# Strips for the modulation rows' products, and an earlier layer boundary, in a two-layer diffusion backbone on one core

## What is computed

```python
for l in range(2):
    mod = silu(c) @ w_mod[l] + b_mod[l]            # 6 x 1024 numbers for each of the two groups
    h = rmsnorm(x) * (1 + mod[1]) + mod[0]
    branches = gmlp(h), conv(h), rwkv_scan(h), attention(h)     # from h @ w_in
    mix = sum_n sigmoid(h @ w_gate[n]) * (branch_n @ w_branch[n]) @ w_out
    x = x + mod[2] * mix
    h = rmsnorm(x) * (1 + mod[4]) + mod[3]
    x = x + mod[5] * moe(h)                        # 16 experts, 2 for each token
y = rmsnorm(x) * final_g
```

## Time and profile before

| | |
|---|---|
| time, median of 3 runs | 2992.97 us (2980.88 to 2995.16) |
| the profiled execution | 2981.84 us, its span 2980.2 us |
| PE busy | 2491.1 us (84%) |
| DVE busy | 1338.7 us (45%) |
| ACT busy | 938.7 us (31%) |
| mean DMA rate | 153 GB/s |
| first product of layer 1 | at 1447.68 us |

### The profile page before, as it was taken

How to read it: one execution, slowest core, us unless ns; L and a number is a source line. 1 busy time by engine, 2 the same in 40 slices (tenths; PEclk the granted TensorE clock), 3 DMA queues, 4 the chain that set the end, 5 groups by cost and what they waited for, 6 DMA issues and landing times. The chain is left out here.

```text
span 2980.2 us, 40890 instructions
## 1 busy us (share of the span) xinstructions
PE 2491.1 (84%) x16436; PEld 1845.7 (62%) x16436; DVE 1338.7 (45%) x1680; ACT 938.7 (31%) x1272; POOL 144.4 (5%) x142
## 2 busy tenths in 40 slices
PE   5998888899987985988569988899889979858880
PEld 2785576667665674777238756676667646747770
DVE  1226433332234644888332283323332255458873
ACT  3122332222121123777221313312222111247771
POOL 0000000100000001000100000001000000010001
PEclk8999899999998996999779998999999989779995
DMA  7117211120113504999532372102111044069984
GB/s 300 57 62 279 93 51 71 70 73 24 64 60 129 209 23 180 395 397 399 230 118 85 122 248 74 72 15 75 69 71 45 35 164 166 29 258 395 395 338 179
DMA packets 75071, 455.78 MB, mean 153 GB/s; under 512 B 8544, under 2 KB 24928, under 8 KB 44384
## 3 DMA queue, kind: packets, MB, share of 16 engines
q1 hardware_dynamic: 57888, 347.10, 30.6%
q0 software_dynamic: 8928, 72.97, 6.5%
q10 hardware_dynamic: 8064, 33.03, 2.7%
HBM read 387.02 MB, written 92.27 MB: 161 GB/s over the span
## 5 line engine op out<-in xcount | busy, mean ns | idle before, releaser
L782 PE MATMUL ps<-h,ring 128*128 128x320 f32 x2048 | 622.6, 455 | 25.0 <-ACT mod_cols L1324 12.8
L782 PEld LDWEIGHTS ps<-h,ring 128*128 128x128 f32 x2048 | 391.9, 197 | 194.9 <-issue 35.5
L782 PE MATMUL ps<-arena 64*64 64x64 f32 (+3 forms) x6608 | 390.0, 249 | 48.2 <-DVE arena L1810 14.3
L782 PEld LDWEIGHTS ps<-arena 64*64 64x64 f32 (+2 forms) x6608 | 297.9, 145 | 169.8 <-issue 135.2
L2041 DVE TENSOR_TENSOR we_lo<-arena,we_hi 128x2048 fp32r<-128x2048 f32 x150 | 339.4, 2290 | 91.7 <-ACT we_hi L1487 91.7
L1487 ACT CAST we_hi<-arena 128x2048 fp32r<-128x2048 f32 x150 | 282.8, 1912 | 2.7 <-DMA arena<-in_experts 2.4
L785 PE MATMUL ps<-fix,arena 128*128 128x128 f32 x836 | 136.1, 308 | 169.3 <-DMA arena<-expert_rows 58.8
L785 PEld LDWEIGHTS ps<-fix,arena 128*128 128x128 f32 x836 | 109.8, 158 | 196.9 <-DVE arena L2071 60.2
L782 PE MATMUL ps<-ring,small 128*2 128x512 f32 x384 | 179.0, 622 | 35.1 <-DMA ring<-in_stream 21.4
L1832 DVE TENSOR_TENSOR arena<-arena,ps 128x512 f32<-128x512 f32 x50 | 34.4, 688 | 355.9 <-PE ps L782 355.9
L782 PE MATMUL ps<-wz_hi,hz_hi 128*128 128x512 f32 (+1 forms) x480 | 181.2, 377 | 15.6 <-DVE hz_lo L1582 15.6
(11 more groups left out here) (286 smaller groups left out, 3399.9 us busy)
## 6 DMA issues: line engine op xcount, KB each, us to landing
arena<-in_experts SPq DMA_DIRECT2D x150, 1024.0 KB, 8.9
ring<-in_stream SPq DMA_DIRECT2D x58, 2048.0 KB, 7.7
arena<-expert_rows SPq DMA_DIRECT2D x50, 512.0 KB, 7.2
expert_out<-rows ACTq DMA_DIRECT2D x50, 512.0 KB, 8.3
gates<-arena SPq DMA_DIRECT2D x128, 160.0 KB, 1.8
ring<-gates SPq DMA_DIRECT2D x16, 1280.0 KB, 5.4
arena<-in_wbranch POOLq DMA_DIRECT2D x2, 3584.0 KB, 12.1
x_kept<-x ACTq DMA_DIRECT2D x2, 2560.0 KB, 15.2
```

What stands on the lines that cost most here:

```text
L782: return nc.tensor.matmul(out, lhsT, rhs, start=start, stop=stop)
```

## The change

It does these things:

- The stationary operand of the modulation products becomes 32 columns wide (`cP`, 2 of them filled, zeroed once), and tile k writes the 32 PSUM partitions of strip k mod 4, so that neighbouring products lie in different column strips of the array. Each strip sums two tiles. ACT copies all 128 partitions; `mod_columns` turns them with a constant `strips` that adds the four strips, a product over 128 rows instead of 2.
- At the start of a layer PE works through all four `w_mod` slots before it turns the first one, and each has its own `mod_row`; ACT copies four times and then adds four biases.
- `cols` and `rows` of the first layer are loaded at once; those of the next layer `cols` after the scatter to the experts and `rows` after the gathers, both on POOL's queue (also after the last layer, where they hold zeros).
- x is stored and squared block by block, behind the addition that completes the block, at the end of the layer before.
- `round_in(1)` and `rest_in(1)` move into the middle of `h_scaled`, and `hz_done` comes in two halves, so that PE needs only the first for the first half slot.
- In the tail the final scale releases one output DMA for each block, and `final_g` is loaded behind `rows`; ACT waits for the last `x_kept` before the root.

```diff
-    "hz_done": 1, "whi_done": 2 * (SLOTS_IN + SLOTS_OUT), "wlo_done": 2 * (SLOTS_IN + SLOTS_OUT),
+    "hz_done": 2, "whi_done": 2 * (SLOTS_IN + SLOTS_OUT), "wlo_done": 2 * (SLOTS_IN + SLOTS_OUT),
...
-    "params_loaded": 2 * 16, "x_kept": 16, "cache_out": 2 * 16, "state_stored": 16, "x_back": 16, "wb0_loaded": 16, "wb1_loaded": 16,
+    "params_loaded": 2 * 16, "x_kept": NB * 16, "cache_out": 2 * 16, "state_stored": 16, "x_back": 16, "wb0_loaded": 16, "wb1_loaded": 16,
...
+cP = sb("silu_c_padded", KT * STRIP)[:, :].rearrange("p (k g) -> p k g", k=KT)
...
-mod_row = combT_t[0:2, 0:512]
+mod_row = [arena[:, 8192 + i * 512:8192 + (i + 1) * 512] for i in range(SLOTS_MOD)] + [combT_t[:, 0:512]] * (MODS - SLOTS_MOD)
...
 def _(pool):
...
+    pool.dma_start(cols[:, :], a["cols"][0]).then_inc(params_loaded, 16)
+    pool.dma_start(rows[:, :], a["rows"][0].broadcast_to([P, NROWS])).then_inc(params_loaded, 16)
...
-        pool.wait_ge(x_done, now.value("x_done", 0))
-        pool.sem_inc(waits_settled, 1)
-        pool.dma_start(cols[:, :], a["cols"][pick].rearrange("o p c -> (o p) c")).then_inc(params_loaded, 16)
-        pool.dma_start(rows[:, :], a["rows"][pick].rearrange("o p c -> (o p) c").broadcast_to([P, NROWS])).then_inc(params_loaded, 16)
...
+        after = bass.ds(layer + 1, 1)
+        pool.dma_start(cols[:, :], a["cols"][after].rearrange("o p c -> (o p) c")).then_inc(params_loaded, 16)
+        pool.wait_ge(params_loaded, now.value("params_loaded", 48))
+        pool.sem_inc(waits_settled, 1)
...
-    pool.wait_ge(x_done, 1 + DEPTH * PER["x_done"])
+        pool.dma_start(rows[:, :], a["rows"][after].rearrange("o p c -> (o p) c").broadcast_to([P, NROWS])).then_inc(params_loaded, 16)
-    pool.wait_ge(final_done, 1)
-    yv = arena[:, 0:NB * D].rearrange("p (b d) -> p b d", b=NB)
-    pool.dma_start(a["y_prompt"], yv[:, 0]).then_inc(cache_out, 16)
-    pool.dma_start(a["y_sample"].rearrange("(b p) d -> p b d", p=P), yv[:, 1:NB]).then_inc(cache_out, 16)
-    pool.wait_ge(cache_out, DEPTH * PER["cache_out"] + 32)
+    for b in range(NB):
+        pool.wait_ge(final_done, b + 1)
+        to = a["y_prompt"] if b == 0 else a["y_sample"][(b - 1) * P:b * P]
+        pool.dma_start(to, xn[:, b]).then_inc(cache_out, 16)
+    pool.wait_ge(cache_out, DEPTH * PER["cache_out"] + NB * 16)
...
 def _(pe):
...
     def mod_rows_products(i, u, bk, ks):
...
-            ins = mm(bank(bk)[0:2, :], cS[:, k, :], slot(u)[:, k, :], k == 0, k == KT - 1)
+            strip = slice(k % 4 * STRIP, (k % 4 + 1) * STRIP)
+            ins = mm(bank(bk)[strip, :], cP[:, k, :], slot(u)[:, k, :], k < 4, k >= KT - 4)
...
-            ins = mm(bank(bk)[:, 2 * j:2 * j + 2], mod_row[:, j * P:(j + 1) * P], ident[0:2, 0:2])
+            ins = mm(bank(bk)[:, 2 * j:2 * j + 2], mod_row[i][:, j * P:(j + 1) * P], fixed("strips"))
...
     def bank_left(what, i):
...
     with pe.Fori(0, DEPTH) as layer:
...
-        pe.wait_ge(slot_loaded[0], now.load(0))
-        mod_rows_products(0, 0, 4, range(KT)).then_inc(mod_mm, 1)
-        for i in range(1, SLOTS_MOD):
+        for i in range(SLOTS_MOD):
...
-            pe.wait_ge(constants_loaded, 3 * 16)
-            mod_columns(i - 1, 3 + i)
-        mod_columns(SLOTS_MOD - 1, 3 + SLOTS_MOD)
+        pe.wait_ge(constants_loaded, 3 * 16)
+        for i in range(SLOTS_MOD):
+            mod_columns(i, 4 + i)
...
-        pe.wait_ge(hz_done, now.next("hz_done"))
...
+                if j == 0:
+                    pe.wait_ge(hz_done, now.next("hz_done"))
...
                 for b in range(NB):
...
-    def squares():
-        for b in range(NB):
-            ins = A(xn[:, b, :], x[:, b, :], ACT.Square, accum_out=ssq[:, b:b + 1])
-        ins.then_inc(ssq_done, 1)
+    def square(b):
+        return A(xn[:, b, :], x[:, b, :], ACT.Square, accum_out=ssq[:, b:b + 1])
+    def keep(b):
+        act.dma_start(x_kept_dram[:, b * D:(b + 1) * D], x[:, b, :]).then_inc(x_kept, 16)
     def squares_behind_w_out():
...
-    def h_scaled(b_at, rounded=None):
+    def h_scaled(b_at, rounded, round_next):
...
+            if f == KT // 2:
+                round_next(1)
...
-            for dst in ([rounded] if rounded is not None else []) + [h]:
+            for dst in (rounded, h):
...
     def mod_row_out(i, bk):
...
-        nc.scalar.copy(mod_row, bank(bk)[0:2, :]).then_inc(mod_rows, 1)
+        nc.scalar.copy(mod_row[i], bank(bk)).then_inc(mod_rows, 1)
     def mod_column_out(i, bk):
...
-    A(cS, cS, ACT.Silu).then_inc(silu_c_done, 1)
+    act.wait_ge(strips_zeroed, 1)
+    A(cP[:, :, 0:2], cS, ACT.Silu).then_inc(silu_c_done, 1)
+    act.wait_ge(x_done, 1)
+    for b in range(NB):
+        ins = square(b)
+        keep(b)
+    ins.then_inc(ssq_done, 1)
     with act.Fori(0, DEPTH) as layer:
-        mod_row_out(0, 4)
-        act.wait_ge(x_done, now.value("x_done", 0))
-        squares()
-        act.dma_start(x_kept_dram, Xt[:, :]).then_inc(x_kept, 16)
...
-        mod_column_out(0, 4)
-        for i in range(1, SLOTS_MOD):
+        for i in range(SLOTS_MOD):
+        for i in range(SLOTS_MOD):
...
-        round_in(1)
-        act.wait_ge(x_kept, now.next("x_kept", 16))
-        h_scaled(0, hz_hi)
+        act.wait_ge(x_kept, now.next("x_kept", NB * 16))
+        h_scaled(0, hz_hi, round_in)
...
+        def after_layer(b):
+            act.wait_ge(x_done, now.value("x_done", b + 1))
+            keep(b)
+            return square(b)
         for b in range(NB):
...
-    act.wait_ge(x_done, 1 + DEPTH * PER["x_done"])
-    for b in range(NB):
-        ins = A(xn[:, b, :], x[:, b, :], ACT.Square, accum_out=ssq[:, b:b + 1])
-    ins.then_inc(ssq_done, 1)
+            if b:
+                after_layer(b - 1)
+        after_layer(NB - 1).then_inc(ssq_done, 1)
+    act.wait_ge(x_kept, (DEPTH + 1) * PER["x_kept"])
...
-        if parts:
-            ins.then_inc(hz_done, 1)
+                if f in (KT // 2 - 1, KT - 1):
+                    ins.then_inc(hz_done, 1)
+                if f == KT // 2 - 1:
+                    rest_in(1)
     def rest_in(v):
...
-        dve.wait_ge(x_kept, now.next("x_kept", 16))
+        dve.wait_ge(x_kept, now.next("x_kept", NB * 16))
-        rest_in(1)
...
-    dve.wait_ge(params_loaded, DEPTH * PER["params_loaded"] + 16)
+    dve.wait_ge(params_loaded, (DEPTH + 1) * PER["params_loaded"] + 16)
     for b in range(NB):
-        ins = V.scalar_tensor_tensor(xn[:, b, :], x[:, b, :], rstd[:, b:b + 1], arena[:, 10240:10240 + D],
-                                     ALU.mult, ALU.mult)
-    ins.then_inc(final_done, 1)
+        V.scalar_tensor_tensor(xn[:, b, :], x[:, b, :], rstd[:, b:b + 1], arena[:, 10240:10240 + D],
+                               ALU.mult, ALU.mult).then_inc(final_done, 1)
...
+    o = FIX["strips"][0]
+    for k in range(4):
+        fix[k * STRIP, o] = fix[k * STRIP + 1, o + 1] = 1.0
...
```

More of the change, by code:

```diff
@@ L45 @@
 SLOT = KT * 512
+STRIP = 32
 OVER = (2 * TOK - NE) // P
@@ L159 @@
                       ("rk", W), ("lnx_g", W), ("lnx_b", W), ("sink", 4), ("br", 20)])
-FIX, NFIX = fields([("ident", P), ("cos", LAT * HD), ("sin", LAT * HD), ("band", 3 * P), ("iota", 4), ("first_row", NE),
+FIX, NFIX = fields([("ident", P), ("cos", LAT * HD), ("sin", LAT * HD), ("band", 3 * P), ("iota", 4), ("strips", 2), ("first_row", NE),
                     ("over_row", NE), ("over_tile", OVER), ("one", 1)])
@@ L326, in build @@
         step_done = sem("step_done")
+        strips_zeroed = sem("strips_zeroed")
         step_mm = sem("step_mm")
@@ L1633, in first_max @@
                 dve.wait_ge(dve_chain, now.next("dve_chain"))
+            V.memset(cP, 0.0).then_inc(strips_zeroed, 1)
             dve.wait_ge(x_loaded, 16)
@@ L2219 @@
         "stream": stream, "wbranch": wbranch, "experts": np.concatenate([up, down], 2),
-        "cols": np.concatenate([cols[n].reshape(L, P, COLS[n][1]) for n in COLS], 2),
-        "rows": np.concatenate([rows[n].reshape(L, 1, ROWS[n][1]) for n in ROWS], 2),
+        "cols": np.concatenate([np.concatenate([cols[n].reshape(L, P, COLS[n][1]) for n in COLS], 2), np.zeros((1, P, NCOLS), np.float32)]),
+        "rows": np.concatenate([np.concatenate([rows[n].reshape(L, 1, ROWS[n][1]) for n in ROWS], 2), np.zeros((1, 1, NROWS), np.float32)]),
         "fix": fix, "scanf": scanf, "scanb": scanb,
```

## The result

| | before | after |
|---|---|---|
| median, 20 runs each on one chip | 2981.93 us | 2963.43 us (2945.21 to 2979.82) |
| ratio, 95% interval | | 0.9937 (0.9915 to 0.9959) |
| the same comparison once more, 11 and 6 runs | 2982.57 us | 2951.74 us, 0.9886 (0.9859 to 0.9913) |
| the profiled execution's span, granted clock | 2980.2 us, 0.918 | 2969.8 us, 0.897 |
| PE busy | 2491.1 us | 2402 us |

The change makes the kernel faster by 0.6% in the first comparison and by 1.1% in the second. The two intervals don't overlap, so one comparison of this kernel is worth about half a per cent whatever its interval says. I take 18 to 31 us as the gain; the forecast was 29.6 us, 2963 for the median.

A forecast was written before the change was run, and what follows sets the result against it. PE was taken to bound most of the span. Start -6, hz +1.4, pairs -1, experts +2, boundary -20, tail -6 sum to -29.6 us, 2981.8 to 2952, or 2963 for the median; range 2938 to 2982.

The forecast's parts named there:

- The start: Start of layer 0: transposes begin sooner through overlapping strips and earlier loads, -6 us, bounds 2 and 11.
- The halves of hz: Layer starts: the wait for the last hT_dve makes the halves worthless, +0.7 us a layer, +1.4 in all.
- The pairs: Behind the branches: 17.7 us gained by strips against 17 us of half clock behind stalls, net -1, bounds -17 and +17.
- The experts: First expert tile: cols loads beside it and delays it, +1 us a layer, bounds 0 and 3.3.
- The boundary: Between the layers: parameters and products ready before x, which comes 6.7 us late; transposes 20 us sooner, bounds 26 and 12.
- The tail: End of the kernel: fewer squares and a smaller last output, -6 us, bounds 4 and 8.
- (1): Modulation products: the strips don't overlap, pairs bring neither gain nor stall; sum -32 us, 2961; 20%.
- (2): Layer boundary: gathers starve, x comes 15 us late and the boundary gives 8; 2975; 14%.
- (3): Pairs behind the branches: half clock costs 5 us a stall, pairs cost 52, sum +24, 3017; 5%.
- (4): Pairs behind the branches: slots' loads don't bind, all 85 us come free and the clock holds, 2879; 4%.

The follow-up runs named there:

- six traces: The six kernels with strips and stalls behind the branches, one trace each; first pair to last gate took 1400.6 to 1414.8 us, mean 1406.5.
- mean of three: Three kernels with the old modulation products behind the branches, one trace each; first pair to last gate took 1401.4, 1410.4 and 1398.8 us, mean 1403.5.
- taking that wait apart: Changed kernel, each w_in product asking for its own bank instead of the transposes ending with a wait for all; ratio 0.9881 to the kernel before.
- `cols` later: Changed kernel, the next layer's cols asked for only after the third expert tile is transposed; ratio 0.9912 to the kernel before.
- holding back the two slots: Changed kernel, slots 4 and 5 (w_in) asked for only when x is complete; ratio 0.9915 to the kernel before.
- taking them out of the way: Changed kernel, gate slot's load behind the branches in two halves, the first asked for after the fourth sigmoid; ratio 0.9654 to the kernel before.

## Why the prediction was right, and where its steps were off

The time was right: 29.6 us forecast, 18 to 31 measured. That the median came out at 2963.43 with 2963 forecast is luck. The forecast started from 2993, the median of three runs of the kernel before; twenty runs give 2981.93, 11 us less, and in that comparison the gain was 18.5 us, also 11 less than forecast. The two errors cancel.

The traces, stage by stage, make it 20.4 us (-7.6 start, +0.9 hz in layer 1, +3.0 pairs, +6.8 experts, -15.9 boundary, -7.6 tail). So three terms (pairs, experts, boundary) were too kind by 13 us together, and two (start, tail) too strict by 4.

- **The start, -6 and +0.7 for hz; measured -7.6 for both.** Nearly the size, by another way. The transposes came 13.2 us sooner, outside my bounds of 2 and 11: the fourth slot was through the queues at 40.5, not 45, since I had put x's whole store ahead of it, and the 32 turn records took 4.14 us in a row, not four times 1.86. But the store then lands last: ACT stands 6.93 us for it, and `w_in` begins 24.2 behind the first transpose, not 19.2. I had counted the store's bytes and not asked who waits for them. The step that failed is "what is late next".
- **The halves of hz, +0.7 a layer.** Layer 1: 19.4 us from the first transpose to `w_in`, against 18.5 before (1525.47 to 1544.00), +0.9. That the last `hT_dve` makes the halves worthless was shown by taking that wait apart: -7.9 us in layer 1.
- **The pairs, -1; measured +3.0, mean of six traces against mean of three, each good to some 7.** Both large terms behind it can be read by themselves. The gains: from the start of a slot's modulation products to the product that follows them, the ten pairs behind the scan take 69.6 us before and 63.8 on the mean of the six, 5.8 less (forecast 7), and the two third pairs 9.7 less (forecast 10.7); the first and second pairs gain nothing. That is 15.5 us, forecast 17.7. The clock: behind the stalls of the first pairs and of the ten the first gate parts are 24.2 us longer on the mean, 2.0 a stall (forecast 17 for these 12, 1.7 in four of five). The difference is a loss of 9 us; the stretch shows 3.0, and its scatter leaves both open. That gain and price nearly cancel is what the change does there, not chance in the sum.
- **The experts, +1 a layer; measured +3.2 and +3.6.** Mis-sized. The bound of 3.3 us, the bytes of `cols` at full rate, was the value itself: I had taken a part of them as free, and none was. `cols` later gave it back.
- **The boundary, -20; measured -15.9** (from the last down product to the transposes 87.5 and 71.7). x came 8.8 us later behind the down products than before, not 6.7: it was the right mechanism, as holding back the two slots showed (8.4 us). From x to the transposes it was 14.0, not 12; 3.8 us in front of DVE's first instruction of the new layer and 2.6 in front of ACT's table load are `issue`, which I hadn't reckoned with. The two run beside each other, so 2.6 us lie on the path. Before, the engines waited for each other at this place, and nothing of that showed on the path. All nine traces with this idle time hold, besides, a transfer of 8 KB on an instruction queue (q14) that starts 2.0 to 2.4 us before DVE goes on, and one that starts 1.6 to 1.7 us before ACT does: at 1510.11 and 1510.69 in the changed kernel, at 1489.07 and 1491.90 with the slots held, where ACT too comes later. So the loading of the loop's first instructions fits; no experiment moved it.
- **The tail, -6; measured -7.6** (27.9 and 20.3 from x complete to the end). I had let the root wait 3.8 us for the last `x_kept`. It did not: the store landed at 2952.19, 2.6 us after its issue, while ACT loaded its table (1.28 us from 2951.37).
- **The rivals.** (1) The strips overlap: 1.92 us a slot. (2) The gathers starve, but by 8.8 us and not 15. (3) The clock decides from 3.3 us a stall; it costs 1.7 to 2.0. The first trace alone would have made a case for it. (4) The slots' loads do bind: taking them out of the way gave 73 us in the stretch. The 84 us that I had put on this rival was about the right price for the wrong kernel.
- The sentence from the Trainium skill's "TensorE: Matmul & The Clock Gate", Part 3, 2.38 times for three column strips: four strips gave 7.03 / 1.92 = 3.7 times here. As foreseen, the sum was the same by either. Its warning against gaps, in "Why this matters for your kernels", agrees with the windows above (0.54 and 0.74 behind the stalls, 1.00 where they are filled), and the price was too small to decide.

## What to carry to other kernels

A product that becomes four times faster is worth only the distance to the next thing that is late: find out what releases the load that stands behind it, and move that release before, or together with, the product. An early release alone and fast products alone brought nothing that can be told from 0 behind the branches here, both together 70 us. And before a few microseconds are read out of a difference between two traces, look at the same stretch in all traces in which it should be the same: here it scattered by 16 us over nine.

## What the runs showed of the hardware

- Four column strips of 32, products of 128 rows by 32 columns on 512 columns in float32: 16 records in 1.92 us at 2.4 GHz, 3.4 to 3.6 us behind a longer idle stretch; one after the other they take 7.03.
- Behind a stall of PE of 4 to 7 us the next 16 records last 2.1 us longer on the mean than the 4.57 us at full clock (12 stalls, 24.9 us, mean of six traces); when other products fill the stalls, the 12 together last 3.0 us longer.
- Ten gathers of 0.5 MB landed 23.6 us after their issue in the middle with four slots of 2 MB beside and behind them, and 14.3 with two.
- At the layer loop's turn DVE and ACT each stand 2.6 to 4.8 us, side by side in part, for nothing that the profile shows. Transfers of 8 KB on an instruction queue start 1.6 to 2.4 us before each of them goes on, in all nine traces that have this idle time; the cause was not tried by itself.
- One stretch of 1400 us with the same work came out between 1398.8 and 1414.8 us in nine executions, and the ratio of one kernel to another at 0.9937 and 0.9886 in two comparisons.
